# Decode attention of a hybrid MLA / S5 decoder step: split-product scores, three-band rotary product, page turns two groups ahead, early first pages

## What is computed

```python
q_lat = jnp.einsum('bqhn,rhn->bqhr', q_nope, w_uk)             # 256 latent channels
ckv_past = ckv_pool[page_table].reshape(B, past, KV_LORA)      # 16 pages of 128 x 256
kpe_past = kpe_pool[page_table].reshape(B, past, D_ROPE)       # 16 pages of 128 x 32
s_past = (jnp.einsum('bqhr,bkr->bhqk', q_lat, ckv_past)
          + jnp.einsum('bqhd,bkd->bhqk', q_pe, kpe_past)).astype(jnp.float32) * scale
...
p = jax.nn.softmax(s, axis=-1).astype(c_kv.dtype)
o_lat = (jnp.einsum('bhqk,bkr->bqhr', p[..., :past], ckv_past)
         + jnp.einsum('bhqk,bkr->bqhr', p[..., past:], c_kv))
```

## Time and profile before

| | us |
|---|---|
| median of 3 runs | 1757.09 (1755.61 to 1760.41) |
| time of the profiled execution | 1761.53 |
| its span, first to last instruction | 1759.9 |
| PE busy (share of the span) | 1555.4 (88%) |
| DVE busy | 716.3 (41%) |
| ACT busy | 571.7 (32%) |
| POOL busy | 327.7 (19%) |
| mean granted clock of TensorE | 0.957 |

### The profile page before, as it was taken

One profiled execution on the slowest core, in us unless ns is written; L12 is line 12 of the kernel. 1 busy time (PEld: TensorE's weight loads), 2 busy tenths in 40 slices (PEclk: granted clock), 3 DMA queues, 4 the chain that ended last, 5 costly groups with the idle time before them and its releaser, 6 DMA issues.

```text
span 1759.9 us, 31391 instructions
## 1 busy us (share of the span) xinstructions
PE 1555.4 (88%) x11270; PEld 1447.2 (82%) x11270; DVE 716.3 (41%) x1070; ACT 571.7 (32%) x969; POOL 327.7 (19%) x359
## 2 busy tenths in 40 slices
PE   6899888788888899999999995239999999999996
PEld 5866666577777799999999995228999999999995
DVE  4765455421222164342344335363444443243332
ACT  6333434443343333321133221204233321133222
POOL 0344535423222001210022300001001210022000
PEclk9998999989999999999999997659999999999998
DMA  7012112512323222222222755800222222222321
GB/s 172 10 41 67 54 52 66 158 32 79 83 57 98 75 73 84 83 84 83 74 82 83 101 120 182 171 7 15 82 82 74 82 86 82 83 79 78 95 61 54
DMA packets 243227, 142.03 MB, mean 81 GB/s; under 512 B 47127, under 2 KB 237518, under 8 KB 242654
## 3 DMA queue, kind: packets, MB, share of 16 engines
q1 hardware_dynamic: 236898, 133.30, 26.8%
q0 software_dynamic: 5872, 7.78, 2.6%
q10 hardware_dynamic: 396, 0.13, 0.0%
HBM read 126.58 MB, written 14.59 MB: 80 GB/s over the span
## 4 chain that ended last, share of the span: by engine, by line
PE 77%; DVE 6%; issue 6%; SPq 5%; ACT 3%; DMA 2%; POOL 0%; DVEq 0%; ACTq 0%; POOLq 0%
PE bank L787 56%; PE bank L702 4%; PE bank L887 4%; SPq L378 3%; SPq L480 2%; PE bank L978 2%; PE bank L837 2%; ACT arena L1224 1%; PE bank L854 1%; PE bank L1168 1%; PE bank L982 1%; PE bank L1162 1%; PE bank L875 1%; PE bank L900 1%; PE bank L894 1%
## 5 line engine op out<-in xcount | busy, mean ns | idle before, releaser
L787 PE MATMUL bank<-arena_parts,wR 128*128 128x288 f32 x4224 | 569.6, 297 | 6.9 <-ACT arena_parts L1293 3.8
L787 PEld LDWEIGHTS bank<-arena_parts,wR 128*128 128x128 f32 x4224 | 565.3, 189 | 9.2 <-issue 6.9
L787 PE MATMUL bank<-side_parts,wR 128*128 128x288 f32 x3360 | 450.2, 296 | 1.1 <-DVE tmpa L2070 1.1
L787 PEld LDWEIGHTS bank<-side_parts,wR 128*128 128x128 f32 x3360 | 448.3, 189 | 1.5 <-issue 1.3
L1638 DVE TENSOR_TENSOR wR<-wraw,wR 128x1024 fp32r<-128x1024 f32 x159 | 232.8, 1464 | 258.5 <-ACT wR L1287 256.9
L1224 ACT ACTIVATE arena<-bank 128x512 f32<-128x512 f32 (+9 forms) x298 | 139.6, 491 | 307.4 <-PE bank L702 126.2
L1287 ACT ACTIVATE wR<-wraw 128x1024 fp32r<-128x1024 f32 x159 | 167.1, 1051 | 211.6 <-PE bank L787 196.4
L664 POOL TENSOR_TENSOR arena_parts<-sq,arena_parts 128x576 f32 x64 | 91.7, 1433 | 681.6 <-ACT arena_parts L1464 681.6
L702 PE MATMUL bank<-ident,arena 128*128 128x128 f32 (+3 forms) x416 | 76.0, 296 | 53.8 <-DMA side<-in_cache_ckv 18.2
L702 PEld LDWEIGHTS bank<-ident,arena 128*128 128x128 f32 (+3 forms) x416 | 49.0, 143 | 78.9 <-DVE arena L1803 21.9
L1461 ACT ACTIVATE tmpa<-bank 128x576 f32<-128x576 f32 x64 | 41.7, 652 | 197.4 <-PE bank L787 197.4
(11 more groups left out here) (249 smaller groups left out, 1393.0 us busy)
## 6 DMA issues: line engine op xcount, KB each, us to landing
wraw<-in_mlp_w SPq DMA_DIRECT2D x128, 512.0 KB, 3.9
side<-in_cache_ckv SPq DMA_DIRECT2D x128, 128.0 KB, 2.1
wraw<-in_ssm_w_glu SPq DMA_DIRECT2D x16, 512.0 KB, 3.9
s_state_to_out<-side SPq DMA_DIRECT2D x16, 256.0 KB, 2.5
s_in_to_state<-yblk SPq DMA_DIRECT2D x8, 512.0 KB, 3.1
wraw<-in_mla_w_o SPq DMA_DIRECT2D x8, 512.0 KB, 5.3
arena<-s_in_to_state SPq DMA_DIRECT2D x1, 4096.0 KB, 12.3
arena<-s_state_to_out SPq DMA_DIRECT2D x1, 4096.0 KB, 12.3
```

Source lines behind the costliest of these rows:

```text
L787: ins = pe.matmul(bank[:, a, 0:HALF], wR[:, s, wp, k, :], tokens(k, xp)[:, a * HALF:(a + 1) * HALF], start=(first and j == 0), stop=(last ...
```

## The change

Three things change in the decode stage, and some loads move.

1. Scores: pages, keys and queries are cut into HI and LO. A group has six fp32r products with 256 columns for the latent part. The rotary part is one fp32r product with 96 rows: `KP3` holds in each page three bands of 32 columns (HI, HI, LO of the keys), turned into `kpT3`; `QP3` has HI, LO, HI of the queries. So a group turns its two pages' keys with two transposes.
2. `turn_pages` runs two groups ahead; `cT` has three places, two of them in `wR`. The first group of the next batch but one is turned within `values`, ahead of the output's turn. In `values` the probabilities' turns alternate with the products, and their copies are shared by ACT (0, 2, 4) and DVE (1, 3).
3. Loads: SP issues two pages of batch 0 in each pass of the pair loop, and POOL four key pages of batches 0 and 1. Block 2 of the output weights is loaded late, since its place holds the keys. In `load_pages` the four page numbers of a quarter are read ahead of its wait.

Work added: ACT cuts the batch's keys (`cut_keys`) and queries (`cut_queries`), ahead of `values`; DVE and POOL make their rests, and DVE the pages' rests (`rest_of_pages`). Some semaphores of the beginning are merged, and a cleared query tile (`QPz`) is gone.

```diff
@@ SP
+            def first_pages(p):
+                for j in range(2):
+                    g = p * 2 + j
...
+                    sp.dma_start(dst, I["cache_ckv"][0][ds(physical(sp, 0, 0, g), 1)].rearrange("o p n -> (o p) n"))\
+                        .then_inc(page0_in, 16)
             with sp.Fori(0, PAIRS - 1) as p:
                 sp.wait_ge(uk_done, p + 1 + CREDIT)
                 apart(sp)
                 pair_weights(p + 1)
+                first_pages(p)
                 chunk_out(p)
-            for m in range(RAW):
+            first_pages(PAIRS - 1)
+            for m in (0, 1, 3):
                 load_block(B_B + m, col(w_o, 0, m))
             def load_pages(i, par):
                 for c in range(4):
+                    at = [physical(sp, i, par, g) for g in range(4 * c, 4 * c + 4)]
                     if not isinstance(i, int):
                         sp.wait_ge(quarter_used, i * 8 + (4 * par + c - 7))
                         apart(sp)
-                    for g in range(4 * c, 4 * c + 4):
-                        sp.dma_start(pages[:, par, g, :],
-                                     I["cache_ckv"][0][ds(physical(sp, i, par, g), 1)].rearrange("o p n -> (o p) n"))\
+                    for j, g in enumerate(range(4 * c, 4 * c + 4)):
+                        sp.dma_start(pages[:, par, g, :], I["cache_ckv"][0][ds(at[j], 1)].rearrange("o p n -> (o p) n"))\
                             .then_inc(page_in[par][c], 16)
-            load_pages(0, 0)
             sp.wait_ge(quarter_used, 4 * (DEC_B - 1))
             sp.dma_start(wkvf[:, :, :], w_kvup).then_inc(wkvf_in, 16)
+            sp.wait_ge(kp3_sb, DEC_B)
+            load_block(B_B + 2, col(w_o, 0, 2))
@@ POOL
+                for j in range(4):
+                    g = p * 4 + j
+                    pool.dma_start(KP0[:, ds(g, 1), :].rearrange("p o n -> p (o n)"),
+                                   I["cache_kpe"][0][ds(physical(pool, 0, 0, g), 1)].rearrange("o p n -> (o p) n"))\
+                        .then_inc(keys0_in, 16)
...
+            for b in range(2):
+                rest_of_queries(b, b)
+            for par in range(2):
+                load_keys(1, par)
+            with pool.Fori(1, DEC_B // 2 - 1) as i:
+                for par in range(2):
+                    rest_of_queries(i * 2 + par, par)
+                    load_keys(i + 1, par)
@@ PE
+                for j in range(2):
+                    transpose(bank23[0:3 * ROPE, 1 - g % 2, j * P:(j + 1) * P],
+                              KP3[:, 2 * g + j, :, :].rearrange("p z n -> p (z n)").bitcast(F32))
...
+                for wp, parts in PASSES:
+                    for xp in parts:
+                        for r in range(2):
+                            rhs = cT[g % 3][:, xp, r, :] if g < 8 else ckvN[:, xp, r, cols]
+                            pe.matmul(bank, QLb[:, par, wp, r, :], rhs, start=first, stop=False)
+                            first = False
+                rhs = kpT3[0:3 * ROPE, g % 3, :] if g < 8 else kpeN3[0:3 * ROPE, cols]
+                ins = pe.matmul(bank, QP3[0:3 * ROPE, par, :], rhs, start=False, stop=(g < 8))
...
+                turn(0)
+                for j in range(4):
+                    turn(j + 1)
+                    probs_turned(j)
+                    for g in range(4 * j, 4 * j + 4):
+                        ins = pe.matmul(bank23[:, 0, 0:256], PT[:, g, :], pages[:, par, g, :], start=(g == 0), stop=False)
+                    ins.then_inc(quarter_used, 1)
...
+                if following is not None:
+                    turn_pages(*following, 0)
                 pe.wait_ge(ol_sb, b + 1)
@@ ACT
+                copy(cT[g % 3][:, HI, :, :].rearrange("p r n -> p (r n)"), bank01[:, g % 2, :]).then_inc(ct_hi, 1)
+                if g % 2 == 0:
+                    copy(kpT3[0:3 * ROPE, g % 3, :], bank23[0:3 * ROPE, 1, 0:256]).then_inc(kt_a, 1)
+            def cut_keys(b, par):
...
+                copy(KP3[:, :, 0:2, :], KP[:, par, :, :].unsqueeze(2).to_broadcast([P, PAGES, 2, ROPE])).then_inc(kp3_hi, 1)
+            def cut_queries(b, par):
+                cols = slice(b * P, (b + 1) * P) if isinstance(b, int) else ds(b * P, P)
+                copy(QP3[0:ROPE, par, :], QPE[0:ROPE, cols])
+                copy(QP3[2 * ROPE:3 * ROPE, par, :], QPE[0:ROPE, cols])
+                copy(QLb[:, par, HI, :, :], QL[:, :, cols]).then_inc(qh_ready, 1)
@@ DVE
+            def rest_of_pages(b, par, g):
+                dve.wait_ge(ct_hi, b * 8 + (g + 1))
+                tt(cT[g % 3][:, LO, :, :].rearrange("p r n -> p (r n)"), bank01[:, g % 2, :],
+                   cT[g % 3][:, HI, :, :].rearrange("p r n -> p (r n)").bitcast(F32), ALU.subtract).then_inc(ct_sb, 1)
+                if g % 2 == 1:
+                    dve.tensor_copy(kpT3[0:3 * ROPE, g % 3, :], bank23[0:3 * ROPE, 0, 0:256]).then_inc(kt_v, 1)
```

More of the change, by code:

```diff
@@ L577, in _ @@
             pool.wait_ge(bb_made, 2)
+            pool.wait_ge(tab_in, 16)
             with pool.Fori(0, PAIRS) as p:
@@ L620, in load_keys, with rest_of_queries @@
                         .then_inc(keys_in[par], 16)
-            pool.wait_ge(tab_in, 16)
-            pool.wait_ge(ca_made, 2 * PAIRS + CREDIT)
-            for par in range(2):
[L625 to L631, removed]
-            for par in range(2):
[L634 to L641, removed]
+            def rest_of_queries(b, par):
+                pool.wait_ge(qh_ready, b + 1)
+                if not isinstance(b, int):
+                    apart(pool)
+                q = QL[:, :, b * P:(b + 1) * P] if isinstance(b, int) else QL[:, :, ds(b * P, P)]
+                pool.tensor_tensor(QLb[:, par, LO, :, :], q, QLb[:, par, HI, :, :].bitcast(F32), ALU.subtract)\
+                    .then_inc(qb_ready, 1)
+            for b in range(2):
+                rest_of_queries(b, b)
+            for par in range(2):
+                load_keys(1, par)
[3 more added lines that the diff above has]
+                    load_keys(i + 1, par)
+            for par in range(2):
+                rest_of_queries(DEC_B - 2 + par, par)
             pool.wait_ge(nat_sb, 5)
@@ L990, in scores, with values, turn @@
             def scores(b, par):
+                turn_pages(b, par, 1)
                 pe.wait_ge(qb_ready, b + 1)
-                pe.wait_ge(qp_ready, b * 4 + 4)
-                turn_pages(b, par, 0)
-                pe.wait_ge(olt_sb, b + (CREDIT - 1) if not isinstance(b, int) else max(b - 1, 0) + CREDIT)
+                pe.wait_ge(qp_ready, b + 1)
                 for g in range(9):
-                    if g + 1 < 8:
-                        turn_pages(b, par, g + 1)
+                    if g + 2 < 8:
+                        turn_pages(b, par, g + 2)
                     group_scores(b, par, g)
-            def values(b, par):
-                pe.wait_ge(d_exp, b + 1)
-                for j in range(5):
+            def values(b, par, following=None):
+                def turn(j):
                     bank = [bank6, bank7][j % 2]
-                    pe.wait_ge(dt_sb, b * 5 + max(j - 1, 0) + CREDIT)
+                    if j == 1:
+                        pe.wait_ge(dt_v, b * 2 + CREDIT)
+                    if j >= 2:
+                        probs_turned(j - 2)
                     if j < 4:
@@ L1437, in _ @@
                 scores(i * 2 + 1, 1)
+                cut_keys(i * 2 + 2, 0)
+                cut_queries(i * 2 + 2, 0)
                 values(i * 2, 0)
@@ L1440, in _ @@
                 scores(i * 2 + 2, 0)
+                cut_keys(i * 2 + 3, 1)
+                cut_queries(i * 2 + 3, 1)
                 values(i * 2 + 1, 1)
@@ L1840, in _ @@
             dve.wait_ge(t_done, 8 * PAIRS + CREDIT)
-            own(dve.memset(QPz[:, :, :, :], 0.0))
-            dve.wait_ge(ql_sb, 4 * PAIRS + CREDIT)
-            settle()
-            def fix_queries(b, par):
-                if not (isinstance(b, int) and b < 2):
-                    dve.wait_ge(sc_done, b * 9 - 9 + CREDIT)
-                for i in range(4):
-                    dve.tensor_copy(QPz[ROPE * i:ROPE * i + ROPE, par, i, :],
-                                    QPE[0:ROPE, b * P:(b + 1) * P] if isinstance(b, int) else
-                                    QPE[0:ROPE, ds(b * P, P)]).then_inc(qp_ready, 1)
```

280 lines of the change are left out of this document (159 added, 121 removed).

## The result

| | before | after |
|---|---|---|
| median of the runs, us | 1758.51 (1755.61 to 1760.41, 4 runs) | 1749.56 (1745.06 to 1753.48, 4 runs) |
| profiled execution, us | 1761.53 | 1753.48 |
| span, us | 1759.9 | 1751.8 |
| mean granted clock | 0.957 | 0.952 |

The account below looks back on a forecast made before the run. SP's page issues were taken to bound the decode loop. Six periods -13, head -6.8 and tail -1.5 made -21.3 us, the clock +1.5: median from 1757.1 to 1737 us, range 1728 to 1750.

Parts of the forecast that it names:

- A: Part of a batch's period from first quarter used to last page landed: 21.2 us, forecast 18.5 by early page numbers.
- B: Part of the period from the last page landed to the start of `values`: 5.8 us, forecast 5.9.
- C: Part of the period from the start of `values` to the first quarter's end: 4.75 us, forecast 5.2 (+0.45).
- period: One batch's loop in the decode stage, A plus B plus C: 31.8 us, forecast 29.6, six times giving -13 us.
- The head: Start of the decode stage, before the first `values`: earlier loads and faster scores were to save 6.8 us.
- PE's road of a batch: TensorE's own work and waits through a whole batch: about 25 us, with SP still ending last.
- TensorE's clock takes some back: I book +1.5: Term in the sum for the whole kernel: a lower TensorE clock was to cost 1.5 us.
- a rival of one chance in seven: Clock falls in each batch behind longer waits for quarters, up to 1.7 us each: 1743-1749 us, chance 0.14.
- the tail, -1.5: Last two value products, without scores: turning beside the products was to save about 0.7 us in each.
- The marker "wrong if C grows past 6 us": Sign against the forecast: the C part of a batch's period exceeding 6 us.

Follow-up runs that it names:

- `x2`: The kernel before with only the four page numbers of each quarter read ahead of its wait: 1743.84 us, ratio 0.9899.
- `x1`: The changed kernel with each page number read right ahead of its own load again: 1770.72 us, ratio 1.006.
- `x6`: The changed kernel with four of the six latent score products of a group, those with the rests, left out: 1742.86 us, ratio 0.9912.
- `x5`: The changed kernel with all sixteen page numbers of a batch read ahead of its first wait: 1727.49 us, ratio 0.9816.
- `x4`: The changed kernel with the next batch's key and query cuts (ACT) and rests (DVE) behind their first copies of the turned probabilities: 1731.93 us, ratio 0.9854.
- `x11`: `x4` with the cut of the next keys ahead of `values` again, only the queries' cut staying later: 1737.34 us, ratio 0.989.
- `x7`: `x5` with the edit of `x4` added: 1710.71 us, ratio 0.9740.

## Why the prediction was off

**Right.** What bounds the kernel: A, B and C and SP between them. Landings still in the chain, issues 0.53 us apart, A 18.6 for 18.5, products 0.118 us apart for 0.12, PE work per period 2.7 us less for 2.5; C 4.89 for a forecast of 5.2, B 6.3 for 5.9, a period 29.85 for 29.6 where the clock holds. `x2` and `x1` give the early numbers 16 and 21 us by the medians, 14.7 and 12.4 between V0 and V6 of their profiles, where 16 were booked, and `x6` shows the score products of four of eight groups to lie off the path. The head gave 6.3 of 6.8: the first score product starts 9.3 us after the last small turn instead of 11.1 (1.8 of the 2.5 forecast). PE's road of a batch, estimated at 25 us with the wait, is 26.15 in `x5`.

**Wrong: the step "TensorE's clock takes some back: I book +1.5".** C priced ACT's later copy as a wait alone, +0.45, with nothing for the clock behind it. The clock was left to a rival of one chance in seven, and that rival put the falls behind the longer waits for pages ("PE now waits 1.9 us, not 1.2, for each quarter"). In after, four of the six falls between V0 and V6 stand behind the wait for ACT's copy in C, and two in B, behind waits of 1.95 and 2.98 us for pages:

```profile
405.68 0.42 PE L740 MATMUL bank<-ident,arena_parts 128*96 128x128 f32 x2 [1.95 <-DMA side<-in_cache_ckv]
563.85 0.66 PE L740 MATMUL bank<-ident,arena_parts 128*96 128x128 f32 x2 [2.98 <-DMA side<-in_cache_ckv]
```

So the rival's price (up to 1.7 us a fall) and its time (1743 to 1749 us) came out nearly right, but mostly by a wait that it did not name; that is luck. The earlier trace rows shows one fall in eight batches, but the stage of before has another, in `scores(1)`, right behind a wait for a copy by ACT, which the prediction does not count:

```profile
377.18 1.37 PE L978 MATMUL bank<-arena 128*128 128x256 f32 x4 [2.41 <-ACT arena L1224]
```

```profile
378.00:381.30 3.30, 3.30 (x14) 3.03 (x13) 0.71 (x2) 0.98 (x2) 1.38 (x3) 0.50 0.04 10
```

The measured term: six periods at 29.85 would be 179.1 us, and they are 190.2, 11.1 more. The falls in C make 6.4 of it (C's excess over 4.89 at V1, V2, V4, V5). Two falls in B, at 406 and 563, make another 2.5, B taking 7.9 and 7.3 us. (That these two belong to the waits ahead of them is read from the trace and was not tried.) A is 18.4 to 18.6 us in four periods, 19.7 in the first, where two page issues took 0.68 and 0.84 us instead of 0.34, and 20.1 in the last, together some 2.5 more. In the last it is a late landing, in the chain of after:

```profile
528.67 2.06 DMA side<-in_cache_ckv
...
560.23 3.57 DMA side<-in_cache_ckv
```

The last page of the last batch takes 3.57 us instead of 2.1 to 2.5 (but 2.08 in `x4`, where the same page went out 16 us earlier). In the window of 561 to 563 after's DMA rows have an instruction load of one packet beside it:

```profile
q8 instruction: 1, 0.02, 2.9%
```

2.9% of 16 engines over 2 us is 0.9 us of one engine. That it held up the packets behind it is an inference; it was not tried.

**Wrong: the tail, -1.5.** I let the turned probabilities' copies save 0.7 us in each of the last two `values`. In the kernel before PE's waits there are only 0.31 and 0.20 us, and the first of these stays. Without a fall the tail is 23.7 us in `x5`, `x4` and `x11`, as before: the interleaving brings nothing. In the profile of after a fall at 583.6 comes on top: eight products of the last batch take 3.34 us instead of 1.99. There PE had waited only 0.64 and 0.61 us for DVE, so a wait of 1.8 us is not needed for a fall.

**What the forecast should have asked.** The extra 1.9 us of ACT work ahead of `values` was priced as +0.45 in C, because PE needs fewer turns before its first product. That holds at full clock (+0.16 measured). But fewer turns and a later copy turn 0.25 us of idle PE into 1.8, and idle PE has a second price, 1.4 to 1.8 us for each batch in which it brings the clock down. The forecast knew of both, the wait in C and the price of a fall, and did not put them together; the rival that came nearest was given too small a chance. The marker "wrong if C grows past 6 us" came true in four of six.

## What to carry to other kernels

Before a faster product is booked, ask who sets the period: here a queue that reads a table entry for each transfer did, and hoisting the reads beat the rewriting of the mathematics; the rewriting paid only after that. Work put ahead of the first copy that TensorE waits for costs twice, as a wait and as a lower clock behind it, so an engine that prepares the next round should do so after it has served the present one. When an engine is waiting more than before, give the clock rival a chance in proportion to the new idle time, not to how rarely the old kernel had such falls.

## What the runs showed of the hardware that I had not expected

- An idle PE can be worth a dummy product. Seven unused products in a wait of 1.8 us kept the clock at 1.00 in the C of six of six batches, where it fell in four of six without them, and gave back 7.5 us.
- Less work for PE can mean more time at low clock: with four of six score products gone the mean clock between V0 and V6 went from 0.94 to 0.89.
- The page numbers' reads stand 0.64 us apart on SP, as the chain of after has them at 454.02 and 454.66, though each table load is 0.27 us long. The Trainium skill (DMA: Bandwidth & Descriptors, Latency and other measured facts) gives a floor of about 600 ns for such a load. This trace doesn't show it: the next register instruction starts 0.30 us after the load does, and it (0.15 us), two shorter ones (0.02 and 0.05) and the gaps between them make up the rest of the 0.64.
- Sixteen transfers of 128 KB issued 0.53 us apart in `x7` land nearly as fast as those of after, which stand 1.1 us apart on average: the median from issue to landing is 2.3 us against 2.1, the longest 4.0 against 3.6. V0 to V6 moves 98 GB/s instead of 76, and landings don't set the pace.
